# Weight loads from ScalarE's queue, other plain pairs, and moved steps in an fp32 encoder layer

## The reference, cut to what matters

```python
h    = rms_norm(x, ln_mix_g)
proj = h @ w_in                                # 1024 -> 5632 columns: u, vg, q, k, v, gates
a    = gelu(u) * (w_s @ layer_norm(gelu(vg)) + b_s)        # per 128 tokens, 8 groups
b    = attention(q, k, v, caches, sinks, window of 128)    # 16 heads, 4 kv heads
gate_a, gate_b = split(sigmoid(gates))
x    = x + (gate_a * (a @ w_pa) + gate_b * (b @ w_pb)) @ w_o
up_a, up_v = split(rms_norm(x, ln_ffn_g) @ w_up)           # 1024 -> 2 * 2816
x    = x + (gelu(causal_conv3(up_a)) * up_v) @ w_down
y    = rms_norm(x, ln_final_g)
```

## Time and profile before

| | |
|---|---|
| median of 3 runs | 1746.06 us (1744.42 to 1748.01) |
| profiled execution | 1745.02 us, its span 1743.2 us |
| PE | 1679.1 us busy, 96% of the span |
| DVE | 1055.9 us, 61% |
| ACT | 661.5 us, 38% |
| POOL | 346.7 us, 20% |
| granted TensorE clock, mean | 0.988 |
| DMA | 209.40 MB, mean 120 GB/s |

### The profile page before, as it was taken

One profiled execution on the slowest core, in us unless ns is written; L12 is line 12 of the kernel. 1 busy time (PEld: TensorE's weight loads), 2 busy tenths in 40 slices (PEclk: granted clock), 3 DMA queues, 4 the chain that ended last, 5 costly groups with the idle time before them and its releaser, 6 DMA issues. The chain is left out here.

```text
span 1743.2 us, 31424 instructions
## 1 busy us (share of the span) xinstructions
PE 1679.1 (96%) x12614; PEld 1625.8 (93%) x12614; DVE 1055.9 (61%) x1828; ACT 661.5 (38%) x1232; POOL 346.7 (20%) x321
## 2 busy tenths in 40 slices
PE   6799999999999897999999999999999999999997
PEld 6798888888889897999999999999999998999997
DVE  6746565565646673242242877777777776666665
ACT  6435444454544333342343544333334332111112
POOL 2321121212113440001222522222222220000001
PEclk9999999999999998999999999999999999999999
DMA  8343434243335756465444122222222226222122
GB/s 250 115 154 107 129 97 133 84 138 95 104 117 174 202 163 220 128 220 161 137 141 143 51 68 82 75 75 75 75 76 87 85 79 238 95 93 97 66 74 104
DMA packets 240579, 209.40 MB, mean 120 GB/s; under 512 B 24759, under 2 KB 197619, under 8 KB 240435
## 3 DMA queue, kind: packets, MB, share of 16 engines
q1 hardware_dynamic: 240206, 207.32, 37.6%
q10 hardware_dynamic: 229, 0.08, 0.0%
HBM read 141.91 MB, written 65.45 MB: 119 GB/s over the span
## 5 line engine op out<-in xcount | busy, mean ns | idle before, releaser
L2053 PE MATMUL ps<-op_hi,w_hi 128*128 128x272 f32 x3248 | 688.8, 293 | 25.9 <-DVE quad L1619 9.1
L2053 PE MATMUL ps<-op_hi,w_lo 128*128 128x272 f32 x3248 | 672.8, 289 | 0.0
L2053 PE MATMUL ps<-op_lo,w_hi 128*128 128x272 f32 x3248 | 672.3, 288 | 0.0
L2053 PEld LDWEIGHTS ps<-op_hi,w_hi 128*128 128x128 f32 x3248 | 510.7, 189 | 53.0 <-issue 48.0
L2053 PEld LDWEIGHTS ps<-op_lo,w_hi 128*128 128x128 f32 x3248 | 512.5, 189 | 0.0
L2053 PEld LDWEIGHTS ps<-op_hi,w_lo 128*128 128x128 f32 x3248 | 509.9, 189 | 0.0
L1512 DVE TENSOR_TENSOR w_lo<-raw,w_hi 128x512 fp32r<-128x512 f32 x224 | 163.6, 746 | 202.9 <-ACT w_hi L1151 202.9
L1151 ACT ACTIVATE w_hi<-raw 128x512 fp32r<-128x512 f32 x224 | 134.8, 626 | 153.6 <-PE ps L2053 128.8
L1958 DVE TENSOR_TENSOR xy<-ps,xy 128x728 f32<-128x728 f32 (+1 forms) x176 | 119.4, 720 | 95.8 <-PE ps L2254 95.8
L994 POOL TENSOR_TENSOR w_f<-raw 128x512 f32<-128x512 f32 x42 | 62.6, 1491 | 566.9 <-PE ps L2053 553.3
L1222 ACT ACTIVATE u<-ps 128x544 f32<-128x544 f32 x84 | 52.2, 621 | 189.0 <-PE ps L2053 189.0
(11 more groups left out here) (168 smaller groups left out, 1657.8 us busy)
## 6 DMA issues: line engine op xcount, KB each, us to landing
in_spill<-quad SPq DMA_DIRECT2D x88, 272.0 KB, 2.2
raw<-in_w_in_dram SPq DMA_DIRECT2D x44, 512.0 KB, 5.4
raw<-in_w_up_dram SPq DMA_DIRECT2D x44, 512.0 KB, 5.0
g_spill<-value_out SPq DMA_DIRECT2D x22, 544.0 KB, 2.7
g_in<-g_spill SPq DMA_DIRECT2D x11, 1088.0 KB, 5.8
d_raw<-in_w_down_dram SPq DMA_DIRECT2D x22, 512.0 KB, 3.4
q_now<-in_spill SPq DMA_DIRECT2D x36, 128.0 KB, 2.4
gate_q<-in_spill SPq DMA_DIRECT2D x16, 272.0 KB, 6.6
```

Source lines behind the costliest of these rows:

```text
L2053: last = pe.matmul(out[:, h, 0:HB], (w_hi, w_lo)[a][place][:, j, :], (op_hi, op_lo)[b][at][:, j, HB * h:HB * h + HB], start=fresh and j == ...
```

## The change

Products and loads:

- Pair 1 becomes plain, pairs 23, 24 and 25 become seven. `lead(g)` is the last pair of the plain run that opens stage g (1, 22, 29, 33 and 34).
- `load_weights(p + 1)` moves from SyncE's list to ScalarE's, to the end of the first slot of pair p (of the second, after `copied`, in a seven pair behind a plain one).
- Of the three loads of the next stage's operand, only `r21` stays at its early point; `r12` and `r22` go behind the first operand at (1, 0) of the stage's last pair, and for stage "pb" the gates go behind them.
- Operand splits of stage "in" are spread over pairs 0 to 2; stage "pb" now needs its sums and all its operands.
- For the stages "out" and "up", part b of operand 1 is split at (6, 2) and (6, 3) of the last pair before, no longer at the start of the stage's first pair. For that `normed` takes the third quadrant one slot earlier.
- `row_factor` goes from (4, 0) to behind the third weight sum at (5, 0); `norm_rows(0)` and `factor_in(0)` move one row tile on.
- At the start of the down product VectorE adds its first block before `value_scale`, and its second before `gated_value`.

```diff
-PLAIN = (0,) + tuple(range(PB, UP)) + (UP,)
+PLAIN = (0, 1, PB) + tuple(range(PA, UP)) + (UP,)
+def lead(g):
+
+    p = FIRST_PAIR[g]
+    while p + 1 < END_PAIR[g] and plain(p + 1):
+        p += 1
+    return p
...
+        def load_weights(engine, p):
+
+            if p:
+                engine.wait_ge(s_w, LOWS_BEFORE[p])
+            view, c1, c2 = weights_of(p)
+            for c, c0 in enumerate((c1, c2)):
+                engine.dma_start(raw[:, c], view[:, :, c0:c0 + P]).then_inc(s_raw, 16)
...
-                    if p + 1 < NPAIR:
-                        load_weights(p + 1)
...
-                        load_operands(g, src)
+                        load_operands(g, src, (1,))
+                    if p == FIRST_PAIR[g] - 1 and (n, j) == (1, 0):
+                        load_first_operand(g, src)
+                        load_operands(g, src, (0, 2))
                         if g == 1:
                             for q in order_of(PB):
                                 load_gate_b(PB, q)
-                    if p == FIRST_PAIR[g] - 1 and (n, j) == (1, 0):
-                        load_first_operand(g, src)
...
-                    if p == 1:
+                    if p == lead(0) + 1:
                         pool.wait_ge(s_xts_out[1], 16 * (NT - 4))
...
-                if p == UP and (n, j) == (4, 0):
-                    row_factor()
...
+                if p == UP and (n, j) == (5, 0):
+                    row_factor()
...
-                if p == 1:
+                if p == lead(0) + 1:
                     act.wait_ge(s_xts_out[1], 16 * (NT - 4))
...
-                            todo = {(3, 0): ((3, "w"),), (5, 0): ((2, "w"),)}.get((n, j), ())
+                            todo = {(3, 0): ((3, "w"),)}.get((n, j), ())
...
                     if (p, g) == (1, 0):
-                        todo = {(0, 2): ((5, "w"),), (0, 3): ((4, "w"),)}.get((n, j), ())
+                        todo = {(5, 0): ((2, "w"),), (6, 1): ((5, "w"),)}.get((n, j), ())
+                    if (p, g) == (2, 0):
+                        todo = {(0, 1): ((4, "w"),)}.get((n, j), ())
...
+                        if (k, j) == ((1, 2) if not plain(p) and plain(p - 1) else (0, 3)) and p + 1 < NPAIR:
+                            load_weights(act, p + 1)
...
-                            lows = {(1, 3): ((0, "a"),), (2, 3): ((1, "a"),), (3, 3): ((0, "b"),), (6, 1): ((7, "a"), (3, "a"))}
+                            lows = {(1, 3): ((0, "a"),), (2, 3): ((1, "a"),), (3, 3): ((0, "b"),), (6, 1): ((7, "a"), (3, "a")), (6, 3): ((1, "b"),)}
...
             taps(FT - 1)
-            value_scale(FT - 1)
-            gated_value(FT - 1)
...
                         last.then_inc(s_added, 1)
+                        if n == 0:
+                            value_scale(FT - 1)
+                        if n == 1:
+                            gated_value(FT - 1)
```

More of the change, by code:

```diff
@@ L605, in load_x @@
                 sp.dma_start(xt[0:rows_of(n), n % XT, :], token_rows(n)).then_inc(s_x_in[n % XT], 16)
-            def load_weights(p):
-                if p:
-                    sp.wait_ge(s_w, LOWS_BEFORE[p])
-                view, c1, c2 = weights_of(p)
-                for c, c0 in enumerate((c1, c2)):
-                    sp.dma_start(raw[:, c], view[:, :, c0:c0 + P]).then_inc(s_raw, 16)
             def store_xt(n):
@@ L621, in _ @@
                 load_x(n)
-            load_weights(0)
+            load_weights(sp, 0)
             for n in range(5, NT):
@@ L647, in stored, with load_operands @@
                     sp.wait_ge(s_q_out[q], 16 * store_count(q, p + 1))
-            def load_operands(g, src):
+            def load_operands(g, src, some):
                 for i, (dst, k, half) in enumerate(((r12, 0, 1), (r21, 1, 0), (r22, 1, 1))):
+                    if i not in some:
+                        continue
                     sp.dma_start(dst[:], src.rearrange("(j k) p t -> k p j t", k=2)[k][:, :, half * QT:half * QT + QT])\
@@ L1155, in operand_hi @@
                 if g or n == 2:
-                    act.wait_ge(s_product, place_freed(first if n == op_place(g, 7) else first - 1, at))
+                    act.wait_ge(s_product, place_freed(lead(g) if n == op_place(g, 7) else first - 1, at))
                 if g == 0:
@@ L1212, in copied @@
                 if plain(p - 1):
-                    act.wait_ge(s_comb, 4 * (p - 1) if p > 1 else 1)
+                    act.wait_ge(s_comb, 4 * (p - 1))
                 else:
                     act.wait_ge(s_comb, comb_count(p - 1, (Q11, Q12, Q21)[i]))
-                if p == 1:
+                if p == lead(0) + 1:
                     act.wait_ge(s_xts_out[1], 16 * (NT - 4))
@@ L1280, in free_place @@
                 kind = stage(p)
-                if kind == "pb":
+                if kind in ("in", "pb") and p:
                     act.wait_ge(s_q_out[q], 16 * store_count(q, p))
@@ L1387, in operands @@
                             todo = {(1, 2): ((0, "a"),), (2, 2): ((1, "a"),), (3, 2): ((0, "b"),), (5, 1): ((7, "a"),),
[L1388 removed]
+                                    (5, 2): ((3, "a"),), (6, 2): ((1, "b"),)}.get((n, j), ())
                     if p == FIRST_PAIR[g]:
                         if g == 0:
[L1391 removed]
+                            todo = {(3, 0): ((3, "w"),)}.get((n, j), ())
                         elif g < 3:
@@ L1434, in background @@
                     sigmoid_a(4 * (p - 1 - PA) + 3)
-                if stage(p) == "out" and j == 1 and n in ((2, 5) if plain(p) else (2, 5, 6)):
+                if stage(p) == "out" and j == 1 and n in ((2, 5) if p == OUT else (2, 5, 6)):
                     normed(4 * (p - OUT) + {2: 0, 5: 1, 6: 2}[n])
                 if OUT < p <= UP and (n, j) == (0, 1):
-                    if plain(p - 1):
+                    if p - 1 == OUT:
                         normed(4 * (p - 1 - OUT) + 2)
@@ L1828, in operands @@
                             sums = {(2, 0): ((0, "b"), (1, "b")), (3, 0): ((2, "w"),)}
-                            lows = {(0, 2): ((1, "b"),), (1, 0): ((7, "b"),), (1, 2): ((6, "a"), (6, "b")), (2, 2): ((3, "b"),),
+                            lows = {(0, 3): ((7, "b"),), (1, 2): ((6, "a"), (6, "b")), (2, 2): ((3, "b"),),
                                     (3, 2): ((2, "w"),), (4, 2): ((5, "w"),), (5, 2): ((4, "w"),)}
                     if (p, g) == (1, 0):
-                        lows = {(0, 2): ((5, "w"),), (1, 0): ((4, "w"),)}
+                        lows = {(5, 2): ((2, "w"),), (6, 2): ((5, "w"),)}
+                    if (p, g) == (2, 0):
+                        lows = {(0, 3): ((4, "w"),)}
                     for i, part in sums.get((n, j), ()):
@@ L1866, in background @@
                 if f == 0:
-                    if (n, j) == (0, 1):
+                    if (n, j) == (0, 2):
                         factor_in(0)
@@ L2006, in product_waits @@
                 g = generation(p)
-                if p == FIRST_PAIR[g] or p == FIRST_PAIR[g] + 1:
+                if p <= lead(g) + 1:
                     pe.wait_ge(s_op, op_count(g, operand))
@@ L2221, in background @@
                     mix_tokens(m)
-                if (p, n, j) == (UP + 1, 0, 0):
+                if (p, n, j) == (UP + 1, 0, 1):
                     norm_rows(0)
```

5 lines of the change are left out of this document (2 added, 3 removed).

## The result

The changed kernel takes **1726.34 us** (median of 4 runs, 1723.53 to 1728.99); the kernel before took 1746.72 in the same session (4 runs). The ratio is 0.9885, 95% interval 0.9864 to 0.9905: faster by 20.4 us. The forecast was 1716.8 with a range of 1705 to 1732, so direction and range hold and the size is 9.5 us too large.

The account below looks back on a forecast made before the run. The prediction took TensorE's matmuls, its stops and the lowered clock behind them to bound the kernel. Its terms summed to -29.3 us: from 1745.0 to 1715.7, plus 1.04 for the median, 1716.8 us, range 1705 to 1732.

Parts of the forecast that it names:

- Products, -5.9: Pairs 1 and 23 to 25: two block products fewer in all, at 2.96 us each, taken whole; -5.9 us.
- Pair 1, -7.9: Pair 1: TensorE's 6.3 us wait for the copy of region 0 and its 1.6 us of clock go; -7.9 us.
- Pair 0, -2.2: Pair 0: without GpSimd's weight sums, two VectorE operations take 1.1 us less each; -2.2 us.
- Pair 21, -4.3: Pair 21: weights asked for earlier, a 5.3 us stop remains where 9.1 was; -4.3 us, bounds -9 and +1.
- Pair 22, "I expect no stop there": Pair 22: operands and sums fill VectorE to about 20 of 24 us, so no stop was expected.
- ScalarE's queue, -4 and +2: Weight loads on ScalarE's queue: pair 18's wait shrinks, -4 us; issues delay ScalarE's steps in pairs 3 to 20, +2 us.
- Row factor, -3.2: Ahead of pair 35: behind the third weight sum the factor costs nobody, VectorE's chain ends about 1 us late; -3.2 us.
- Down product, -2.3: Start of the down product: first addition goes earlier, 4.1 us stop shrinks to about 1.8, some clock returns; -2.3 us.
- Start of pair 34, -1.5: Start of pair 34: the stop for the lo part of operand 1, part b, moves into the previous pair's slack; -1.5 us.
- the queue doesn't matter: Rival, chance 0.15: transfers share the bandwidth, not the queue; pairs 18 and 21 keep their stops; 1725 us.
- ScalarE becomes the gate: Rival, chance 0.14: issues hold ScalarE 1.5 to 2 us, stopping TensorE in up and attention pairs; 1730 to 1740 us.
- it gives more: Rival, chance 0.12: pairs 18 and 21 lose their stops wholly and ScalarE's issues cost nothing; 1707 us.

Follow-up runs that it names:

- values_early: Changed kernel with ScalarE making the second of three values in pair 1 instead of at the first tick of pair 2; 1726.59 us (ratio 0.9892).
- raw_sums: Changed kernel with pair 22's weights landing before SyncE issues the operand loads, and pair 21's two full-size sums behind the quadrant; 1729.00 us (0.9911).
- normed_old: Changed kernel with ScalarE's third norm step of pair 33 put back at the start of pair 34; 1723.34 us (0.9877).
- sp_queue: Changed kernel with SyncE issuing the weight loads again, at the start of the pair before; 1727.38 us (0.9893).
- raw_first: Changed kernel with SyncE issuing a stage's first operand, `r12`, `r22` and gates only after the next pair's weights have landed; 1726.51 us (0.9889).
- pb_plain: Changed kernel with pairs 23 to 25 plain again, so that stage "pb" makes no sums; 1731.25 us (0.9919).
- sums_late: Changed kernel with VectorE's two full-size sums of pair 21 put behind the quadrant that TensorE's last product waits for; 1726.40 us (0.9881).
- row_old: Changed kernel with GpSimd's row factor put back at the fifth product of pair 34, ahead of the third weight sum; 1726.73 us (0.9888).
- two_plain: Changed kernel with pairs 22 and 23 plain, sums and operands spread over both, weights landing first, the norm's step put back; 1718.23 us (0.9852).
- tail_old: Changed kernel with `value_scale` and both parts of `gated_value` put back ahead of the down product's first additions; 1729.50 us (0.9904).

## Why the prediction was right, and where its sum was off

It was right in sign and range, and -29.3 us became -20.4. That the time lies inside the range is in part luck. In the table the terms miss by 23 us to the slow side (pair 21 alone 9.8, pairs 34 and 35 6.6, pair 2 4.0) and by 10 to the fast side (pairs 17 to 20, the cost of ScalarE's issues, the down product, pairs 26 to 33), and these cancel in part. By its own steps:

- **Products, -5.9.** Right: one more in pair 1, three fewer in pairs 23 to 25, and the page of after has the 3 x 3232 = 9696 matmuls that were expected at L2071. Pairs 22 to 25 gave 7.7 of 8.9 us, since pair 25 has a stop of 0.82 us and its clock.
- **Pair 1, -7.9.** Right, to 0.1 us: 33.24 - 28.33 = 4.9, and 3.0 for the added product. Wrong was the sentence behind it, that the next late thing is operand 4 in pair 2 and has 20 us: `v_tok` was late from 3.2 us after pair 2's start, a wait that the prediction did not list. ScalarE's second value stands behind three hi parts, one of which waits for a weight sum of GpSimd that took 3.38 us. That cost 2.7 to 4.0 us, and values_early shows that two further waits lie just behind it.
- **Pair 0, -2.2.** The stop shrank by 2.0 us (3.20 to 1.17), and for the reason given: the sum of 3.53 us takes 2.42, and the two lo parts behind it 4.76 for 6.75. The pair as a whole gave only 0.8: after has 0.64 of clock at 32 to 36 us where before had 0.99. The eleven other profiles with after's code there go with it, from 30.27 us at a clock of 0.52 (raw_sums) to 29.05 us at 0.94 (normed_old), 1.9 below before at nearly before's clock. What decides the clock at the start stayed open.
- **Pair 21, -4.3.** This is the step that failed most: +5.5 in the profiled pair, +3.2 to +5.5 over the repeats, so 7.5 to 10 us of the forecast. "Weights landed at 10 to 11" was wrong: they landed at 20.1 us. The request moved from 5.4 to 2.3 us into the pair, and the landing from 19.1 to 20.1. The 7 to 8 us from request to landing stood on no row of engines as full as these; what they had to move then (the weights, three operands and four gates, at 348 to 389 GB/s) was the same as before, and my upper bound of +1 asked whether an operand would be late, never whether the weights would. sp_queue and raw_first show it: 9.8 and 9.4 us from request to landing when they go first, 17.8 when they share. After, the operands were late too (`r12` at 16.9 us and `r22` at 20.4, past the sign of 16 us), but nobody waited for them, since the weights stand first in the lists of ScalarE and VectorE. The list of VectorE behind the landing I had counted rightly: 12.1 us from the landing to the end of the quadrant, for 12.7 to 13.7 predicted; pb_plain takes two operations away and the stop is 5.1 us shorter. In the sum itself stands a slip of 0.4 us: 23.7 - 18 is 5.7, not 5.3.
- **Pair 22, "I expect no stop there".** True after, because the stop of pair 21 came first and gave VectorE its time. Taken away, it reappears: 4.6 us in sums_late and in raw_sums. The estimate of 20 of 24 us left out that VectorE's operations stretch beside GpSimd's: in both the sum in pair 22 took 6.79 us and two lo parts 3.51 each, where such operations take 2.42.
- **ScalarE's queue, -4 and +2.** Right in direction, too small and too large: 8.4 us given in pairs 17 to 20 and nothing paid that shows. The term had only the stop of pair 18; the waits for `vg_t` and `gs` went with it, 3.1 us in all. In the up stage the issues lie under a running ACTIVATE. The stated upper bound of +20 also doesn't follow from 1 us for each of 36 pairs, which is 36. The rule that I weighed against this term (the Trainium skill, DMA: Bandwidth & Descriptors, Issuing engines are not separate DMA queues) would have made it 0. Its premise shows in pair 21, where the loads of both queues share full engines, and not in the 0.99 us that the prediction set beside it, which shows only how short an issue is. Its conclusion doesn't hold for this kernel, since 8.9 to 9.9 us of pairs 17 to 20 come and go with the queue.
- **Row factor, -3.2.** The step itself gave 2.3 to 2.6, or 1.0 against the two longer profiles (row_old). It doesn't show in pairs 34 and 35, because two steps that I had costed as gains or at nothing work against it in the same pair: the norm's step moved into pair 33 costs 1.4 to 1.8 us (normed_old), and the stop taken from pair 34 returns ahead of pair 35. From the last quadrant of pair 33 on VectorE to the first product of pair 35 it is 27.0 us before (977.19 to 1004.21), 25.4 after (967.53 to 992.92) and 25.3 in two_plain. The chain is 1.6 us shorter, but that quadrant, which stood 3.5 us into pair 34 before, stands 6.9 us into it after and 5.3 us in normed_old and two_plain. That chain sets the start of pair 35, wherever TensorE stands meanwhile. For what delays the quadrant by the other 1.8 us (the moved operand part is a candidate) no kernel was run alone.
- **Down product, -2.3.** Right in mechanism: waits of 1.8 us in all after, as predicted; the size was 2.6 to 3.8 by tail_old, since I gave the clock back only in part and it stayed at 1.00.
- **Start of pair 34, -1.5.** The stop shrank from 1.53 to 0.95 us and is not kept, as above. The same move of a part b in stage "out" I had not costed: before, TensorE waited 0.62 us for a lo part at 883.41, in pair 30; after, this wait is gone and pairs 26 to 33 are 0.8 us shorter.

Of the rivals, "the queue doesn't matter" had the nearest time (1725) by luck: pair 21 kept its stop, as it said, but pair 18 didn't, and the queue moved both; "ScalarE becomes the gate" is refuted by the constant 21.05 us; "it gives more" was right for pairs 17 to 20 alone.

## What to carry to other kernels

When a load is asked for earlier, ask what else is in the DMA engines then: its landing is set by the bytes that go before or beside it, and a queue of its own makes it share with everything, where a place ahead in one queue would let it pass first. A stop that is taken away gives back only what the engine behind it has to spare: add up that engine's list over the next two stages, not over the one with the stop. And when an edit moves the same median by nothing, look at the length of the stretch that it touches before calling it worthless; here two effects of 5 to 10 us cancelled.

## What the runs showed of the hardware

**A DMA issue can be free on ScalarE.** 1.01 us of issues (1232.69) lie beside an ACTIVATE of 1.30 us (1232.66) on the same engine, and pairs 36 to 55 kept their 421.2 us.

**GpSimd's full-size operation stops VectorE's.** The parts of 0.71 and 2.42 us that took 5.42 and 6.58 have two inputs in SBUF and began while GpSimd read two others; VectorE's sum at 976.43 us after took 7.11 us beside one of 5.45. The Trainium skill (SBUF — State Buffer, Who interferes with whom) states such an exclusive hold by whichever of the two began first; the trace agrees, with 965.13 + 4.87 = 970.0 and VectorE's end at 970.6. The price belongs in every sum of VectorE's list: GpSimd's time there is VectorE's time too.

**The same stop has two prices.** In pair 2 TensorE waits 2.47 to 2.49 us for `v_tok` in eleven profiles. In seven of them the granted clock from 92 to 96 us is 1.00 and the pair takes 24.7 us, in four it is 0.59 to 0.73 and the pair takes 25.9 to 26.1.
